# A decoder trunk with two experts layers: the pace of the experts' dot products beside the delta nets' chains

## What is computed

```python
h = rmsnorm(x, norm_mix_g[i]) * (1.0 + sc1) + sh1
m = gla_mixer(...) if i % 2 == 0 else gdn_mixer(...)
x = x + gt1 * m
h = rmsnorm(x, norm_ffn_g[i]) * (1.0 + sc2) + sh2
x = x + gt2 * peer_ffn(h, ...)
```

```python
ue = jnp.take(u, ib, axis=0)
act = gb * jax.nn.gelu(jnp.einsum('nd,nkd->nk', tb, ue))
ve = jnp.take(v, ib, axis=0)
return jnp.einsum('nk,nkd->nd', act, ve)
```

## Time and profile before

| | |
|---|---|
| median of 3 executions | 1930.27 us (1926.15 to 1933.41) |
| profiled execution, its time | 1927.03 us |
| its span in the trace | 1925.2 us |
| PE busy | 1529.6 us, 79% |
| DVE busy | 1334.0 us, 69% |
| moved by DMA | 703.32 MB, mean 365 GB/s |
| delta net of tile 0 (w = 1), read from the trace | 600 to 1095 us |
| delta net of tile 1 (w = 2) | 1098 to 1590 us |

### The profile page before, as it was taken

How to read it: one execution, slowest core, us unless ns; L and a number is a source line. 1 busy time by engine, 2 the same in 40 slices (tenths; PEclk the granted TensorE clock), 3 DMA queues, 4 the chain that set the end, 5 groups by cost and what they waited for, 6 DMA issues and landing times.

```text
span 1925.2 us, 22276 instructions
## 1 busy us (share of the span) xinstructions
PE 1529.6 (79%) x7828; PEld 912.6 (47%) x7828; DVE 1334.0 (69%) x3962; ACT 418.5 (22%) x1139; POOL 583.4 (30%) x551
## 2 busy tenths in 40 slices
PE   6999999965656889888889687998889875555555
PEld 6644876511113656666558265766656641111111
DVE  6667646769976779585446776877845579778654
ACT  1221211000002722622211264154121210000001
POOL 0110223444442322322222322232232244444541
PEclk8999798667678989999899898999998987886887
DMA  9988499999998967987999998699699999999995
GB/s 368 360 319 308 183 402 376 411 422 421 421 421 356 421 270 273 421 317 277 393 409 417 391 398 321 223 388 373 232 385 396 421 379 403 421 421 421 422 422 227
DMA packets 100255, 703.32 MB, mean 365 GB/s; under 512 B 15264, under 2 KB 15648, under 8 KB 16560
## 3 DMA queue, kind: packets, MB, share of 16 engines
q0 software_dynamic: 78336, 570.46, 73.6%
q1 hardware_dynamic: 21808, 131.45, 17.0%
HBM read 700.82 MB, written 1.05 MB: 365 GB/s over the span
## 4 chain that ended last, share of the span: by engine, by line
PE 43%; DMA 20%; DVE 15%; issue 5%; ACT 5%; POOL 1%; SPq 0%; DVEq 0%; POOLq 0%; ACTq 0%
PE PS L1646 15%; DMA vb<-in_peer_uv,idx 8%; DMA ub<-in_peer_uv,idx 6%; PE PS L1796 3%; PE PS L1702 3%; PE PS L2013 3%; PE PS L1989 3%; DMA ring<-in_peer_uv,idx 2%; DVE vb L1147 2%; PE PS L1970 2%; DVE ub L1147 2%; PE PS L1749 2%; PE PS L1873 1%; ACT ring L1472 1%; DMA mods<-in_peer_uv,idx 1%
## 5 line engine op out<-in xcount | busy, mean ns | idle before, releaser
L1646 PE MATMUL PS<-ub,z 128*64 128x512 f32 x832 | 342.7, 762 | 128.4 <-DVE z L1113 125.0
L1646 PE MATMUL PS<-vb,z 128*64 128x512 f32 x828 | 318.4, 748 | 106.9 <-DVE z L1113 105.2
L2046 POOL DMA_INDIRECT ub<-in_peer_uv,idx x208 | 227.4, 1093 | 522.4 <-PE PS L1646 458.2
L2046 POOL DMA_INDIRECT vb<-in_peer_uv,idx x207 | 230.8, 1115 | 434.9 <-PE PS L1646 389.2
L1359 ACT ACTIVATE tanhs<-cubed 128x2 f32<-128x2 f32 x256 | 52.0, 203 | 879.0 <-DVE cubed L1102 855.5
L1646 PEld LDWEIGHTS PS<-ub,z 128*64 128x64 f32 x832 | 77.8, 162 | 279.0 <-DVE z L1113 184.4
L1646 PEld LDWEIGHTS PS<-vb,z 128*64 128x64 f32 x828 | 73.7, 160 | 262.9 <-DVE z L1113 170.4
L1147 DVE CUSTOM_DVE_ANT_0 vb<-vb,h 128x1024 f32<-128x1024 f32 x104 | 127.1, 1222 | 54.0 <-DMA vb<-in_peer_uv,idx 53.4
L1646 PE MATMUL PS<-mods,z 128*64 128x512 f32 x204 | 124.8, 743 | 36.9 <-DVE z L1113 34.5
L1147 DVE CUSTOM_DVE_ANT_0 ub<-ub,h 128x1024 f32<-128x1024 f32 x104 | 127.1, 1222 | 35.7 <-DMA ub<-in_peer_uv,idx 33.6
L1106 DVE SCALAR_TENSOR_TENSOR acts<-tanhs,gated_x 128x2 f32<-128x2 f32 x256 | 40.4, 158 | 152.4 <-ACT tanhs L1359 146.1
(11 more groups left out here) (364 smaller groups left out, 2780.2 us busy)
## 6 DMA issues: line engine op xcount, KB each, us to landing
ring<-in_gdn_qkv SPq DMA_DIRECT2D x32, 1024.0 KB
ring<-in_peer_wq SPq DMA_DIRECT2D x23, 1024.0 KB
two_slots<-in_ada_wide POOLq DMA_DIRECT2D x20, 1024.0 KB, 7.8
ring<-in_gdn_z SPq DMA_DIRECT2D x16, 1024.0 KB
ring<-in_gdn_w_out SPq DMA_DIRECT2D x16, 1024.0 KB
ring<-in_gla_w_in SPq DMA_DIRECT2D x6, 2048.0 KB, 11.0
mods<-in_ada_wide POOLq DMA_DIRECT2D x11, 1024.0 KB, 7.5
ring<-in_ada_w SPq DMA_DIRECT2D x4, 2048.0 KB, 11.9
```

The source lines that it names most:

```text
L1646: last = pe.matmul(y[64 * g:64 * g + 64, e, :], z[:, i % 4, g, :], rows[:, D + e * 512:D + (e + 1) * 512], start=False, stop=False, skip_g ...
L2046: pool.indirect_dma_start(row_buffers[b], None, uv_rows, off).then_inc(row_landed[b].sem, 16)
```

## The change

`dot_at` gets a table, PACE, for the stretches w = 1 and 2: of the 128 dots 17 stand up to place 86, 28 in the first core (86 to 164), 15 in the second weights (to 236), 28 in the second core (to 314) and 40 in the tail. Even spacing had 21, 19, 18, 19 and 51. Stretches 0 and 3 keep theirs. The second edit gives ScalarE's wait for the last product of the state (`ds_done`) a place of its own, 14.5 steps behind the start of the carry, where it had stood directly behind the copies of the outputs at 10.

```diff
             W_AT = (0.0, A, A + B, A + 2 * B, 2 * A + 2 * B)
 
+            PACE = ((0.0, 0), (86.0, 17), (164.0, 45), (236.0, 60), (314.0, 88), (B, STRETCH))
+
             def dot_at(w, n):
-                return W_AT[w] + (W_AT[w + 1] - W_AT[w]) * (n + 1) / STRETCH
+
+                if w in (0, 3):
+                    return W_AT[w] + A * (n + 1) / STRETCH
+                (at, of), (to, upto) = next((a, b) for a, b in zip(PACE, PACE[1:]) if n + 1 <= b[1])
+                return W_AT[w] + at + (to - at) * (n + 1 - of) / (upto - of)
...
                                     act.activation(o_of(t)[:, hf * HH + gq * GRP:hf * HH + (gq + 1) * GRP, :], core.ps("O", gq), ACT.Copy).then_inc(o_out.sem, 1)
+                                yield core.at("U", 0) + core.dt * 14.5
                                 act.wait_ge(ds_done.sem, ds_count(t, hf, last_of(t), 1))
```

## The result

The changed kernel is slower: 1966.97 us median of four executions (1959.38 to 1970.15) against 1931.3 of the kernel before in the same comparison, a ratio of 1.0195 with a 95% interval of 1.0172 to 1.0218. The forecast was 1908, the range 1880 to 1942. The profiled execution took 1967.87 us, its span is 1966.0.

What follows compares the result with a forecast made beforehand. Arithmetic was taken to bind the cores and mostly transfers the other stages: cores pay 41 us, other stages save 63, sum -22 from the profiled 1927.0 to 1905, plus 3.3 for the median: forecast 1908, range 1880 to 1942.

Steps and rivals of the forecast that it cites:

- What bounds the kernel: Whole kernel: arithmetic binds in the four cores (DMA share 0.67 to 0.78), mostly transfers elsewhere (0.93 to 0.98).
- I keep this surplus: Four cores: time over the busier engine's work stays 10.8, 9.5, 11.0 and 9.2 us, giving 41 us more.
- Work in the cores: Four cores: a moved pair adds 1.94 us on PE and 2.82 on DVE, a search piece 1.0 on DVE.
- Second weights: Second weights stages: two pairs fewer each save 7.5 us each, 15 in all, with PE running almost without a gap.
- the sign of 10 or less: Second weights: the 18 us of transfer on the chain should shrink to 10 or less.
- Tails: Two tails: five pairs fewer each save 20 us each, 40 in all, four fifths of the transfers' price; some 176 us each.
- First weights: First weights stages: two pairs fewer each save PE's price only, 4 x 1.94 = 8 us, since buffers are full by then.
- Transfers inside a core: Cores of w = 1: added transfers fit, 74 us within 85.8 and 80 of 95.6, so buffers can end full.
- less than 25: First core: POOL's 51 us of waits should shrink below 25.
- Second edit: ScalarE's wait given its own place: costs 0; if late, a few us once or twice.
- A: Cores: engines take turns, 4.21 us a pair, cores pay 88, kernel 1955; with what lies toward C, chance 0.20.
- The rule of the Trainium skill: Cores: by weight loads pairs cost PE 10 us, DVE alone binds, cores pay about 34 instead of 41; not adopted.

Runs made afterwards that it cites:

- slack for PE: Changed kernel with PE's pairs in stretches 1 and 2 placed two dots later (n + 4 instead of n + 2): 1948.14 us, ratio 1.0088.
- half pairs: Changed kernel with the matmuls of pairs placed in a core 256 columns wide instead of 512, results not the kernel's: 1938.88 us, ratio 1.0062.
- half dots: Changed kernel with dots placed in a core taken over 512 of 1024 numbers, results not the kernel's: 1925.71 us, ratio 0.9986.
- The run with 24 pairs a tail: Changed kernel with 23 dots in each core instead of 28 (table 19, 42, 59, 82), no added slack: 1924.51 us, ratio 0.9977.
- the half runs: Changed kernel with dots in the cores half as wide, 1925.71 us, and with pairs' matmuls in the cores half as wide, 1938.88 us.
- the run with slack in the cores: Kernel before with PE's pairs two dots later in the cores alone (places 86 to 164 and 236 to 314): 1912.66 us, ratio 0.9909.
- the moved searches: Changed kernel with two blocks' searches moved out of the first core of w = 1 and second core of w = 2: 1954.17 us, ratio 1.0105.

## Why the prediction was wrong, step by step

- **What bounds the kernel**: right in its two halves, transfers idle in the cores and bind elsewhere. What it left out is that a denser core lets the engines wait for each other, so its idle transfers can't be had for the price of the engines' work.
- **"I keep this surplus"** is the step that failed. I priced the cores by the work of the busier engine plus the 9 to 11 us over it, 41 us in all; they took 82. By the windows above the work rose by 51 and the surplus by 31. My ground, that the surplus did not grow in the second core of w = 2 where DVE was nearly as busy, was drawn from pieces of searches on DVE that no PE instruction waits for. A dot is waited for by the pair, and the pair stands in front of the level's products. The earlier trace rows had both on the chain; there PE's work filled the level all the same, and only the change broke that. In the changed kernel slack for PE took 28 us off the cores (18 to 19 off those of the kernel before), half pairs 35 and half dots 24 to 40. Up to 13 of the 82 are the clock, which no term of my sum held.
- **Work in the cores**: DVE's 2.82 us a pair hold: by the windows its work rose by 64 us for 18 pairs and 12 pieces, against 63. PE's 1.94 hold only at a granted clock of 1.00; PE's work rose by 45 us, not 35, since more pairs ran at 0.50. That, and the other cut, are why the windows give 51 us where I had 41. The pieces cost about what I said, and moving them gained 13 us in the kernel.
- **Second weights**: 15 us expected, 16.1 measured. PE now runs through them without a gap, 45.22 and 45.25 of 46 us by the windows, which I had named as the condition. Part of the gain is the clock: it was 1.00 in both, and PE had been busy at 0.50 for 8.6 us there before, worth up to 4 us. On the chain of w = 2 no transfer is left in this stage. On that of w = 1 one of 20.46 us stands at its end (816.27 us) and reaches 5 us into the second core, so there the sign of 10 or less failed.
- **Tails**: 40 expected, 28.6 measured; 176 us each expected, 181 and 179 measured. The run with 24 pairs a tail suggests the shape: the first two pairs a tail gave 5.2 us each, near their transfers' 4.98, the next three 1.3. In the tail of w = 1 DVE's waits for rows fell from 16.4 to 5.2 us (9.6 with 24 pairs), so little more was to be had there from fewer dots; what bounds the tail then I did not trace.
- **First weights**: 8 expected, nothing measured (0.6 us longer). I had taken PE's work off, but it hardly fell: the granted clock of these stages was 0.88 and 0.86 after against 0.95 and 0.90 before by the new cut, and PE was busy at 0.50 for 28.1 us instead of 17.5, worth up to 5 us. The rest stays open.
- **Transfers inside a core**: they are hidden, as I said, by a core much longer than I said. POOL waits there even more than before, 43.4 + 28.2 us for PE in the first core of w = 1 against 26.1 + 24.8, not less than 25: nine full buffers do not help where buffers come back slowly.
- **Second edit**: nothing lost, right (alone it gained some 4 us); that the pace can't do without it I had not seen.
- **The rivals**: A came nearest: all four cores grew by over 17 us with the engines waiting for each other, and 88 us for the cores stood against 82 measured. Some of that nearness is luck. Up to 13 of the 82 are the clock; the half runs put two thirds to three quarters of a pair's price on the chain and not all of it; "neither is full" did not hold before, where PE filled the levels; and its place, the levels, is not what decides, since 28 dots a core with the extra ones outside the levels cost the kernel as much. Its time, 1955, was 12 too low since it took my 63 us saved where 44 came. The rule of the Trainium skill (page "Perfetto Trace Analysis", section "Identifying the Most-Contended Engine"), by which the matmuls' busy share is no good measure of how near PE is to its limit and the weight loads' share is one, would have made the cores cheaper: "about 34" us, 33 by the terms above. The trace does not bear it out here: in the run with slack in the cores the chain is PE's matmuls without a gap, 17.00 of 17 us, while the weight loads fill 13.51 of them and DVE 15.18:

```profile
845.00:862.00 17.00, 17.00 (x130) 13.51 (x130) 15.18 (x38) 0.61 (x3) 3.75 (x4) 1.00 0.80 296
```

What stays open: the division of the loss at pace 28 into dots ahead of L1282 and into z for the pairs in head and carry, where slack did not help; how much of the 13 us of the moved searches belongs to which stage; and why the clock was lower in some runs.

## What to carry to other kernels

Where two engines take turns on a chain and both run in strict order, extra work between the turns is priced nearer to the sum of what it takes on both (here 1.94 + 2.3 us a pair, of which some two thirds were found on the chain) than by the busier engine; before filling an idle resource beside such a chain, ask which engine's order the work stands in and who is behind it. A consumer placed directly behind its producer in program order has no slack: two dots of it took 18 us off the kernel before (12 with every pair kept in its core), and only where no one was short of the buffers it holds longer. When work is moved between stages, the gain per piece is the resource's price only until the next bound is reached: move in two or three sizes (20, 23 and 28 dots here) before believing a slope. And put the granted clock beside every stage that is compared: here it was up to 16 us of a difference of 40.

## What the runs showed that I had not expected

The best version, 23 dots a core and two dots of slack from head to levels, takes 1906.92 us, 1.0% less than the kernel before (0.9899, 0.9865 to 0.9932). Rival A had named a pair whose z is not yet made, but nothing in the prediction asked whether PE could stand further behind it. Half as wide a dot takes 0.685 us instead of 1.22, and half as wide a pair 1.08 instead of 1.94, so they keep a fixed part of 0.15 and 0.22 us. And the loss is almost the same in both directions from the even pace, +1.8% with 15 dots a core and +2.0% with 28, by opposite causes: late rows there (40 us of DVE's waits in one tail), longer cores here.
